# Attention kernel: the layout of the value tiles and the order of a key pair's products

## What is computed

```python
def blocked_gqa(q, k, v):
    ...
    def one_block(qblk):
        s = jnp.einsum('bqkgd,bskd->bkgqs', qblk, k, preferred_element_type=jnp.float32)
        p = jax.nn.softmax(s.astype(jnp.float32), axis=-1).astype(v.dtype)
        return jnp.einsum('bkgqs,bskd->bqkgd', p, v)
```

## Time and profile before

| | us |
|---|---|
| median of three runs | 1677.11 |
| the profiled execution, its own time | 1678.19 |
| its span from the first to the last instruction | 1676.2 |
| PE busy in the span | 1562.2 (93%) |
| DVE, ACT, POOL busy | 1033.2, 808.2, 516.1 |

### The profile page before, as it was taken

One profiled execution on the slowest core, in us unless ns is written; L12 is line 12 of the kernel. 1 busy time (PEld: TensorE's weight loads), 2 busy tenths in 40 slices (PEclk: granted clock), 3 DMA queues, 4 the chain that ended last, 5 costly groups with the idle time before them and its releaser, 6 DMA issues. The chain is left out here.

```text
span 1676.2 us, 21346 instructions
## 1 busy us (share of the span) xinstructions
PE 1562.2 (93%) x7069; PEld 1248.5 (74%) x7069; DVE 1033.2 (62%) x1484; ACT 808.2 (48%) x1014; POOL 516.1 (31%) x281
## 2 busy tenths in 40 slices
PE   4898884999999999999999999999999999979998
PEld 1787772777777777777777777777887888868886
DVE  3677875778787877878778787862200073265543
ACT  2555431667766666676667666672101122432121
POOL 2323330445445454554545455462000000000000
PEclk8899995999999999999999999999999999999999
DMA  9455437000000000000000000007643105276661
GB/s 357 154 166 163 156 104 234 32 22 16 22 16 25 22 16 22 16 23 21 20 22 16 22 16 25 22 7 198 221 174 126 44 20 218 93 162 186 192 179 75
DMA packets 104597, 151.93 MB, mean 91 GB/s; under 512 B 9497, under 2 KB 73025, under 8 KB 103138
## 3 DMA queue, kind: packets, MB, share of 16 engines
q1 hardware_dynamic: 97650, 138.57, 26.6%
q0 software_dynamic: 6672, 12.58, 2.5%
q10 hardware_dynamic: 224, 0.09, 0.0%
HBM read 104.95 MB, written 46.27 MB: 90 GB/s over the span
## 5 line engine op out<-in xcount | busy, mean ns | idle before, releaser
L711 POOL TENSOR_TENSOR prob_lo<-prob,prob_hi 128x1024 fp32r<-128x1024 f32 x128 | 310.3, 2424 | 415.2 <-ACT prob L744 415.2
L782 DVE TENSOR_REDUCE chunk_max<-max_ps 128x1 f32<-128x512 f32 (+1 forms) x640 | 395.6, 635 | 66.2 <-PE max_ps L856 60.9
L743 ACT ACTIVATE prob_hi<-s_ps 128x1024 fp32r<-128x1024 f32 x288 | 295.2, 1025 | 230.0 <-PE s_ps L874 229.9
L744 ACT ACTIVATE prob<-s_ps 128x1024 f32<-128x1024 f32 x288 | 293.6, 1020 | 0.0
L856 PE MATMUL max_ps<-k_hi,blk_q_hilo 128*128 128x512 f32 (+1 forms) x640 | 248.0, 390 | 30.0 <-DVE chunk_max L782 17.2
L873 PE MATMUL s_ps<-blk_q_hilo,k_hi 128*128 128x512 f32 x576 | 233.3, 405 | 1.1 <-DVE blk_q_negm L798 0.8
L894 PE MATMUL hi_ps<-prob_hi,v_hl 128*128 128x512 f32 x576 | 227.5, 395 | 2.3 <-POOL prob_lo L711 2.2
L874 PE MATMUL s_ps<-blk_q_negm,k_lo 65*128 65x512 f32 x576 | 229.3, 398 | 0.0
L896 PE MATMUL lo_ps<-prob_lo,v_one 128*128 128x512 f32 x576 | 228.6, 397 | 0.0
L895 PE MATMUL lo_ps<-prob_hi,zero_one 128*128 128x512 f32 x576 | 227.0, 394 | 0.0
L804 DVE TENSOR_TENSOR prob_lo<-prob,prob_hi 128x1024 fp32r<-128x1024 f32 x160 | 198.3, 1239 | 23.7 <-ACT prob L744 23.7
(11 more groups left out here) (215 smaller groups left out, 2198.1 us busy)
## 6 DMA issues: line engine op xcount, KB each, us to landing
w_mod<-in_w_mod SPq DMA_DIRECT2D x8, 1024.0 KB, 16.1
x<-in_x SPq DMA_DIRECT2D x8, 1024.0 KB, 5.7
h_scratch<-h_hi SPq DMA_DIRECT2D x8, 1024.0 KB, 4.6
h_scratch<-h_lo SPq DMA_DIRECT2D x8, 1024.0 KB, 7.1
q_scratch<-q_hilo SPq DMA_DIRECT2D x16, 512.0 KB, 3.6
blk_q_hilo<-q_scratch SPq DMA_DIRECT2D x32, 256.0 KB, 2.8
hh<-h_scratch SPq DMA_DIRECT2D x4, 2048.0 KB, 10.7
hl<-h_scratch SPq DMA_DIRECT2D x4, 2048.0 KB, 16.0
```

Of the source, the lines that this page charges most:

```text
L711: nc.gpsimd.tensor_tensor(prob_lo[slot3(j)][:], prob[slot3(j)][:], prob_hi[slot3(j)][:].bitcast(F32), ALU.subtract).then_inc(s_lo_pool, 1)
L743: nc.scalar.activation(prob_hi[slot3(j)][:], s[:], ACT.Exp)
L744: nc.scalar.activation(prob[slot3(j)][:], s[:], ACT.Exp).then_inc(s_exp, 1)
L782: last = nc.vector.reduce_max(chunk_max[:, qt, kc:kc + 1], bank[:, 0:MAX_CHUNKS[kc]], X_AXIS)
```

## The change

The values now lie in two other tiles. `v_one` holds the high part of v in columns 0 to 63 and ones in columns 64 to 127 from the start, and is used with both parts of the probabilities, into one bank (`o_ps`, shown as att_ps). `v_lo` holds the low part of v in columns 0 to 63 and a zero in column 64, 65 columns in all, and is used with the high part, into the bank `lo_ps`. The rows of both banks agree, so the output of a block is one sum of two 65-row tiles. `zero_one`, `hi_sum`, `part` and the two additions on POOL go.

```diff
-            def pv(b, slot, kvh, j, e):
-                if j == 0 and e == 0:
-                    pe.wait_ge(s_hisum, b + 1)
-                    pe.wait_ge(s_losum, b + 1)
...
-                nc.tensor.matmul(hi_ps[:], k.v_hl[:, kt, kvh, :], hi, start=first, stop=final)
-                nc.tensor.matmul(lo_ps[:], k.zero_one[:], hi, start=first, stop=False)
-                last = nc.tensor.matmul(lo_ps[:], v_one[:, kt, kvh, :], lo, start=False, stop=final)
-                if e == 1:
-                    last.then_inc(s_pv, 1)
+            def pv_hi(b, slot, kvh, j):
+                if j == 0:
+                    pe.wait_ge(s_att, b + 1)
+                pe.wait_ge(s_exp, b * PAIRS + (j + 3))
+                for e in range(2):
+                    kt = 2 * j + e
+                    hi = prob_hi[slot3(j)][:, e * QB:(e + 1) * QB]
+                    first, final = kt == 0, kt == KT - 1
+                    nc.tensor.matmul(o_ps[:], k.v_one[:, kt, kvh, :], hi, start=first, stop=False)
+                    last = nc.tensor.matmul(lo_ps[0:HD + 1, :], k.v_lo[:, kt, kvh, :], hi, start=first, stop=final)
+                if j == PAIRS - 1:
+                    last.then_inc(s_pvhi, 1)
+
+            def pv_lo(b, slot, kvh, j):
+                if j in POOL_LO:
+                    pe.wait_ge(s_lo_pool, b * len(POOL_LO) + (POOL_LO.index(j) + 1))
...
+                for e in range(2):
+                    kt = 2 * j + e
+                    last = nc.tensor.matmul(o_ps[:], k.v_one[:, kt, kvh, :], prob_lo[slot3(j)][:, e * QB:(e + 1) * QB],
+                                            start=False, stop=kt == KT - 1)
+                last.then_inc(s_pv, 1)
...
-                    here = [(pv, b, slot, kvh, j, e) for e in range(2)]
+                    here = [(pv_hi, b, slot, kvh, j), (pv_lo, b, slot, kvh, j)]
```

The end of a block, on ACT and on DVE, and what POOL loses:

```diff
-            def evacuate(b, slot):
-                act.wait_ge(s_pv, b * PAIRS + (PAIRS + 3))
...
-                act.wait_ge(s_hisum, b + 1)
-                nc.scalar.activation(part[:], hi_sum[HD:P, :], ACT.Copy).then_inc(s_part, 1)
+            def evacuate(b):
+                act.wait_ge(s_pvhi, b + 1)
+                act.wait_ge(s_att, b + 1)
+                nc.scalar.activation(lo_sum[:], lo_ps[0:HD + 1, :], ACT.Copy).then_inc(s_losum, 1)
...
             def evacuate(b, slot):
                 dve.wait_ge(s_pv, b * PAIRS + (PAIRS + 3))
-                dve.wait_ge(s_att, b + 1)
-                nc.vector.tensor_copy(hi_sum[:], hi_ps[:]).then_inc(s_hisum, 1)
+                dve.wait_ge(s_st[slot], (b - slot) * 16 + 32)
+                dve.wait_ge(s_losum, b + 1)
+                nc.vector.tensor_tensor(att[slot][:], o_ps[0:HD + 1, :], lo_sum[:], ALU.add).then_inc(s_att, 1)
...
-                nc.gpsimd.tensor_tensor(att[slot][:], hi_sum[0:HD, :], lo_sum[slot][0:HD, :], ALU.add).then_inc(s_add, 1)
...
-                nc.gpsimd.tensor_tensor(att[slot][:], att[slot][:], part[:], ALU.add).then_inc(s_att, 1)
```

The constant columns are now set by POOL in the first stage, and DVE's two instructions at the head of the attention go:

```diff
             head_gain(0, 0, True)
+            nc.gpsimd.memset(k.v_one[:, :, :, HD:P].bitcast(F32), 1.0).then_inc(k.s_vone, 1)
+            nc.gpsimd.memset(k.v_lo[:, :, :, HD:HD + 1].bitcast(F32), 0.0).then_inc(k.s_vone, 1)
...
-            nc.vector.memset(v_one[:, :, :, HD:P].bitcast(F32), 1.0)
-            nc.vector.tensor_copy(v_one[:, :, :, 0:HD], k.v_hl[:, :, :, 0:HD].bitcast(F32)).then_inc(s_vone, 1)
```

More of the change, by code:

```diff
@@ L119, in project_qkv @@
         sin_t = [sb(f"sin{i}", [P, 2, HD]) for i in range(2)]
-        q_hilo = [sb(f"q_hilo{i}", [P, HQ, P], F32R) for i in range(2)]
+        q_hilo = [nc.alloc_sbuf_tensor_at(f"q_hilo{i}", [P, HQ, P], F32R, offset=o)
+                  for i, o in enumerate((k.gate_at, k.gate_at + 4 * D))]
         xt_ps = [ps(f"xt_ps{i}", [P, 2, W]) for i in range(2)]
@@ L413, in head_norm @@
                 dve.wait_ge(s_vhi, t + 1)
[L414 removed]
+                nc.vector.tensor_tensor(v_lo, v, v_hi.bitcast(F32), ALU.subtract).then_inc(s_v, 1)
                 dve.wait_ge(s_hsum, t + 1)
@@ L629, in attention @@
                    for i in range(3)]
[L630 to L634, removed]
+        lo_sum = sb("lo_sum", [HD + 1, QB])
+        att = [sb(f"att{i}", [HD + 1, QB]) for i in range(2)]
         max_ps = [ps(f"max_ps{i}", [P, QB]) for i in range(2)]
         s_ps = [ps(f"s_ps{i}", [P, 2 * QB]) for i in range(2)]
-        hi_ps = ps("hi_ps", [P, QB])
+        o_ps = ps("att_ps", [P, QB])
         lo_ps = ps("lo_ps", [P, QB])
@@ L774, in _ @@
             dve.sem_inc(s_mfree, 2)
-            nc.vector.memset(hi_sum[:], 0.0).then_inc(s_hisum, 1)
+            dve.sem_inc(s_att, 1)
             def reduce(b, slot, u):
@@ L877, in scores @@
                     last.then_inc(s_score, 1)
-            def pv(b, slot, kvh, j, e):
-                if j == 0 and e == 0:
-                    pe.wait_ge(s_hisum, b + 1)
-                    pe.wait_ge(s_losum, b + 1)
-                if e == 0:
-                    pe.wait_ge(s_exp, b * PAIRS + (j + 3))
-                    if j in POOL_LO:
-                        pe.wait_ge(s_lo_pool, b * len(POOL_LO) + (POOL_LO.index(j) + 1))
-                    else:
-                        before = sum(1 for m in range(j) if m not in POOL_LO)
-                        pe.wait_ge(s_lo_dve, b * (PAIRS - len(POOL_LO)) + (before + 1))
-                kt = 2 * j + e
-                q = slice(e * QB, (e + 1) * QB)
-                hi, lo = prob_hi[slot3(j)][:, q], prob_lo[slot3(j)][:, q]
-                first, final = kt == 0, kt == KT - 1
-                nc.tensor.matmul(hi_ps[:], k.v_hl[:, kt, kvh, :], hi, start=first, stop=final)
-                nc.tensor.matmul(lo_ps[:], k.zero_one[:], hi, start=first, stop=False)
-                last = nc.tensor.matmul(lo_ps[:], v_one[:, kt, kvh, :], lo, start=False, stop=final)
-                if e == 1:
-                    last.then_inc(s_pv, 1)
@@ new lines, in pv_lo @@
+            def pv_lo(b, slot, kvh, j):
+                if j in POOL_LO:
+                    pe.wait_ge(s_lo_pool, b * len(POOL_LO) + (POOL_LO.index(j) + 1))
+                else:
+                    before = sum(1 for m in range(j) if m not in POOL_LO)
+                    pe.wait_ge(s_lo_dve, b * (PAIRS - len(POOL_LO)) + (before + 1))
+                for e in range(2):
[3 more added lines that the diff above has]
+                last.then_inc(s_pv, 1)
@@ L1562, in build @@
             k.value_at = (nc.sbuf_base + 31) // 32 * 32
-            k.v_hl = sbi("v_hl", [P, KT, HKV, P], F32R)
+            k.v_one = sbi("v_one", [P, KT, HKV, P], F32R)
+            k.v_lo = sbi("v_lo", [P, KT, HKV, HD + 1], F32R)
             with ExitStack() as first:
```

43 lines of the change are left out of this document (13 added, 30 removed).

## The result

The changed kernel takes 1679.63 us (median of 20 runs, 1678.74 to 1682.18) against 1677.39 for the kernel before (20 runs, 1674.55 to 1679.7). The ratio is 1.0014, with a 95% interval of 1.0008 to 1.0021: about 2.2 us slower, inside the 0.2% that the prediction called no change, at its upper end. The forecast was 1681.5, or +4.4 us, twice what came, with a chance of 0.58 for "slower" and 0.27 for "same": the less likely of the two came, and 1679.63 lies at the lower end of the forecast's own bounds (1679 to 1684). The profiled execution took 1679.77 (span 1677.8), 1.58 more than the one of before.

The account below looks back on a forecast made before the run. PE's list of matmuls was taken to bound the attention, with a gap before use 5 in each block. Terms 7.0 - 1.5 - 1.1 = +4.4 us gave 1681.5 us, range 1673 to 1688.

Parts of the forecast that it names:

- Order inside a pair: Pair 0: use 2 one matmul later, gap before use 5 grows 0.70 to 0.93 us, +7.0 us over 30 blocks.
- Narrower load: PE's load of 65 columns takes some 135 ns, beside a running matmul of 0.233 us either way: 0 us.
- rival 2: At the 576 v_lo products, the narrower load brings the next start forward: 18 ns each, 10 us, 1671; 12%.
- End of a block: ACT's copy starts two products earlier, DVE's addition ends at 722.1 before PE needs the banks at 722.46: 0 us.
- POOL loses two additions, and nobody on the way to the end waited for them: At a block's end, removing POOL's two additions frees nothing awaited except at the very end: 0 us.
- main term: The longer gap before use 5 in 30 blocks, 0.233 us each: +7.0 us, with no work seen to hide it.
- Last block: PE's waits for low parts before pairs 2, 4 and 6 shrink from 3.8 to about 2.3 us: -1.5 us.
- attention to tail: From PE's last attention product to the first tail product, the 1.09 us wait for ACT's signal goes: -1.1 us.
- First block, head and first stage: First-block low part ends with POOL's, head's first maximum starts no sooner, POOL's 2.3 us of memset is covered: 0 us.
- Rival 1: At a block's end POOL's low part holds up DVE's addition to 722.65: +10 us, 1691.7; 10%.
- Rival 3: The gap before use 5 does not grow, as low part 1 hangs on pair 1's exponentials: 1674.5; 10%.
- Rival 4: Changing between 65 and 128 output rows empties PE's array, 0.16 us 1152 times: +184 us, 1865; 3%.

Follow-up runs that it names:

- place of the use: Changed kernel with the third use of each pair behind 2, 3 or 5 products instead of four: 1667.26, 1672.21 and 1697.47 us.
- place of the low part: Changed kernel with LO_AFTER[0] = 1, DVE doing low part 1 ahead of the maximum of use 2: 1664.38 us, ratio 0.9917.
- the order alone without the second addition: Kernel before with the new order inside a pair, POOL's second addition (att + part) left out: 1681.56 us, ratio 1.0026.
- the run with the 128-column tile: Changed kernel with a 128-column tile of v_one in place of v_lo's 65 columns: 1681.62 us, ratio 1.0021.
- the layout alone: Changed kernel with the old order of products inside a pair: 1680.51 us, ratio 1.0011.
- the order alone: Kernel before with only the new order, both high products of each half first, then the two low ones: 1711.67 us, ratio 1.0198.
- the kernel before with three edits: Kernel before with third use behind two products, low part 1 ahead of use 2's maximum, table with one use less in pair 0: 1666.21 us.
- behind 5 products: Changed kernel with the third use of each pair behind five products instead of four: 1697.47 us, ratio 1.0115.
- the fastest kernel: Changed kernel with third use behind two products, low part 1 ahead of use 2's maximum, one use less in pair 0: 1650.93 us.

## Why the prediction was right or wrong

*Order inside a pair, +7.0.* Right in place, chain and mechanism. From the scores product to use 5 the distance grew from 0.934 to 1.169 us in the mean of the 30 blocks, by 0.235 where 0.233 was forecast (idle 0.55 to 0.78), and the two ways of moving the cause, place of the use and place of the low part, moved the gap. The blocks as a whole grew by 0.199 each, 5.98 us in all. The rest went in the dense distances beside the gap, 0.2326 us in the mean against 0.2331, a small shift that the prediction's bounds had allowed 1 us for. The narrow tile doesn't explain it: the order alone without the second addition grew by only 0.185 us a block, with all tiles 128 columns wide. What shortens these distances stays open.

*Narrower load, 0.* Nothing measured speaks clearly against it. At most it is the 0.041 us a block of the run with the 128-column tile, 1.2 us in 30, or 2.3 ns a product and not the 18 of rival 2; that run doesn't show that the load is the cause. One argument against rival 2 was wrong: 0.117 us is less than the 189 ns of a 128-column load, but not "less than any load takes", since the prediction's own row has one of 82 ns. The load itself came out as estimated (135 ns):

```profile
L864 PEld LDWEIGHTS lo_ps<-prob_hi,v_lo x576: 134/135/228, 295.0 to 1142.6; 128*65 128x65 f32 x192
```

*End of a block, 0.* Right, with less to spare than written. The addition starts 0.14 behind ACT's copy rather than "some hundredths", 0.3 and not 0.15 behind the last product, and ends 0.24 us before PE wants the bank, not 0.36. With one product less of lead that is gone, as the layout alone shows.

*"POOL loses two additions, and nobody on the way to the end waited for them".* This step was wrong as reasoning, and that its 0 us was right is luck. Nobody waited for them, but the second runs into low part 1, which it starts 0.13 to 0.22 us behind, and the new order moves the low part past it. With the additions left in, the order alone cost 1.67 us a block in its trace and 33 us by the median. I looked for waits on the removed work, and not for what the moved work would meet. The main term of +7.0 holds only because the change that moves the low part also removes the addition that it would have met.

*Last block, -1.5; attention to tail, -1.1.* Together -3.31 measured against -2.6. The passage to the tail is exact: 1.09 us before, 0 now. The waits in the last block shrank by 2.2 us instead of 1.5, within the bounds. Pair 2 no longer waits, as forecast; the two waits that are left, for the low parts of pairs 4 and 7, lose 0.6 us each with their restart, where 1.0 and 0.9 were forecast. Order alone accounts for 1.3 of the 2.2 (29.15 against 30.45), layout alone for 0.7 (28.76 without its 0.13 at the passage, against 30.45 without 1.09), probably because the exponentials come earlier without `part`.

*First block, head and first stage, 0.* -0.04 and 0; the scatter of the first stage is larger than anything the memsets could add. In the first block of before DVE's low part ended at 301.70, 1.09 us behind POOL's at 300.61 and not with it; either way the maximum ahead of it didn't count.

*Rival 1 (addition held by POOL)* falls: 0.69 us in all 32 blocks, 31 of them with POOL's low part running. The Trainium skill ("SBUF — State Buffer", Who interferes with whom) has a DVE instruction with one SBUF input free of POOL, and this trace agrees. *Rival 3 (chain on the exponentials)* falls for this kernel, but the exponentials are what low part 1 waits for once the uses are moved, in the kernel before with three edits. *Rival 4* falls: the distance from the 65-column product to the next is 0.232 us in the mean of the 540 in the 30 blocks, that of its neighbours.

The changed kernel was forecast 1.9 us above its median: 1.0 from the main term and 0.7 from the end of the attention; the rest is scatter.

## What to carry to other kernels

When an order moves by one matmul, ask not only who waits for it but what the moved work now starts beside: here a DVE and a POOL instruction 0.1 us apart decided by their order who lost about 1 us. Halves of a change must not be priced apart and added: here the order alone cost 33 us, the layout alone 2, and both together 2, because each takes away what makes the other dear. And the stall in this ring of two buffers was moved most cheaply by the order of the reader, one number in a table here, worth more (15 us) than the change itself.

## What the runs showed of the hardware

- When DVE's low part and POOL's addition, both with two SBUF inputs, met, one kept its time (1.22 or 1.28 us) and the other took about 1 us more. With POOL 0.05 to 0.10 us ahead it was always DVE that lost; with rows 0.01 or 0.02 apart DVE lost in 13 of 14 blocks. DVE's addition with one operand in PSUM kept its 0.69 us beside POOL.
- A wait of PE costs more than its idle time. In the kernel before 0.55 us are idle, but use 5 starts 0.70 late, since dense rows overlap, and the next start comes another 0.1 late, behind a row of 0.50 instead of 0.40. So several short waits (behind 5 products: three more, 0.45 us a block) cost more than one a little longer.
- A wait shorter than the overlap shows no idle time at all. In every one of these traces the first scores product behind the broadcast starts 0.36 to 0.38 us after its forerunner, and the next one 0.33 after it, in the fastest kernel too, where PE was busy 400.00 of 400 us. PE's list has waits there, and the row, here of the fastest kernel, is 0.50 long like one behind a wait:

```profile
730.07 0.50 PE L849 MATMUL s_ps<-blk_q_hilo,k_hi 128*128 128x512 f32 x1
```

- A load of 65 columns took 135 ns and one of 128 took 189, and products started 0.232 to 0.233 us apart behind either.
- Gaps of 1.8 us in every block of 28 us brought the granted clock down to 0.50 (1.2 GHz) in eight of the 30 middle blocks; gaps of 0.9 us (behind 5 products) did so in none of them.
